# Expert products moved from split operands of 96 slots to plain fp32 in column groups of 128-slot rounds, with the final norm formed slot by slot

## The reference, cut to what matters

```python
lg = xt @ router_group;  le = xt @ router_expert        # group, then top 2 of its 8 experts
for e in range(N_EXPERTS):                              # 32 experts, D 1024, FF 256
    hdn = silu(xt @ w_gate[e]) * (xt @ w_up[e])
    y = y + comb[:, e:e + 1] * (hdn @ w_down[e])
y_prompt = rmsnorm(h + y, norm_final)[:, N_META:]       # and y_sample
```

## Time and profile before

| | us |
|---|---|
| median of 3 runs | 1011.46 (1009.23 to 1011.9) |
| the profiled execution, its own time | 1011.97 |
| its span, first to last instruction | 1010.1 |
| PE busy in the span | 917.7 |
| DVE busy | 595.2 |
| ACT busy | 503.5 |
| POOL busy | 234.6 |
| moved by DMA | 203.92 MB |

### The profile page before, as it was taken

One profiled execution on the slowest core, in us unless ns is written; L12 is line 12 of the kernel. 1 busy time (PEld: TensorE's weight loads), 2 busy tenths in 40 slices (PEclk: granted clock), 3 DMA queues, 4 the chain that ended last, 5 costly groups with the idle time before them and its releaser, 6 DMA issues. The chain is left out here.

```text
span 1010.1 us, 13905 instructions
## 1 busy us (share of the span) xinstructions
PE 917.7 (91%) x4971; PEld 725.2 (72%) x4971; DVE 595.2 (59%) x1051; ACT 503.5 (50%) x870; POOL 234.6 (23%) x304
## 2 busy tenths in 40 slices
PE   3899999999999999987899999499999999999962
PEld 3799887888878887775678776377777777777621
DVE  4503533253324432366685336888999999888756
ACT  4523344334443434334332212568888888888614
POOL 1102223233213322202452201211011011010435
PEclk9999999999999999998699999689999999999977
DMA  8032221321232122317145534999999999999976
GB/s 250 38 109 77 89 73 52 96 78 58 74 114 72 54 74 75 120 32 226 64 138 180 177 125 180 358 314 385 388 394 394 398 398 393 400 401 373 350 276 229
DMA packets 88363, 203.92 MB, mean 202 GB/s; under 512 B 11903, under 2 KB 55231, under 8 KB 76006
## 3 DMA queue, kind: packets, MB, share of 16 engines
q1 hardware_dynamic: 77806, 169.99, 47.4%
q0 software_dynamic: 5984, 17.18, 5.1%
q10 hardware_dynamic: 4504, 15.85, 4.1%
HBM read 167.02 MB, written 39.99 MB: 205 GB/s over the span
## 5 line engine op out<-in xcount | busy, mean ns | idle before, releaser
L1017 PE MATMUL pj<-n_hi,w_hi 128*128 128x350 f32 (+1 forms) x576 | 199.2, 346 | 3.5 <-DVE n_lo L1337 3.5
L1017 PE MATMUL pj<-n_lo,w_hi 128*128 128x350 f32 (+1 forms) x576 | 188.5, 327 | 0.0
L1017 PE MATMUL pj<-n_hi,w_lo 128*128 128x350 f32 (+1 forms) x576 | 187.6, 326 | 0.0
L1941 DVE TENSOR_TENSOR e_lo<-e_raw,e_hig 128x2048 fp32r<-128x2048 f32 x64 | 145.9, 2282 | 0.0
L1017 PEld LDWEIGHTS pj<-n_hi,w_hi 128*128 128x128 f32 x576 | 109.9, 191 | 35.4 <-issue 33.6
L1299 DVE CUSTOM_DVE_ANT_0 sc<-pj,strip 128x512 f32<-128x512 f32 (+5 forms) x120 | 60.9, 544 | 119.0 <-PE pj L1083 78.0
L1937 ACT ACTIVATE e_hig<-e_raw 128x2048 fp32r<-128x2048 f32 x64 | 122.5, 1918 | 10.3 <-DMA e_raw<-in_w_up 9.6
L1017 PEld LDWEIGHTS pj<-n_lo,w_hi 128*128 128x128 f32 x576 | 110.2, 191 | 0.6
L1017 PEld LDWEIGHTS pj<-n_hi,w_lo 128*128 128x128 f32 x576 | 109.8, 191 | 0.9 <-issue 0.8
L1989 PE MATMUL pj<-e_hig,xT_hi 128*96 128x512 f32 x256 | 104.8, 410 | 0.0
L1989 PE MATMUL pj<-e_hig,xT_lo 128*96 128x512 f32 x256 | 101.3, 396 | 0.0
(11 more groups left out here) (291 smaller groups left out, 1637.5 us busy)
## 6 DMA issues: line engine op xcount, KB each, us to landing
e_raw<-in_w_up SPq DMA_DIRECT2D x32, 1024.0 KB, 16.7
e_raw<-in_w_gate SPq DMA_DIRECT2D x32, 1024.0 KB, 20.7
e_raw<-in_w_down SPq DMA_DIRECT2D x32, 1024.0 KB, 21.2
w_raw<-in_w_in SPq DMA_DIRECT2D x24, 512.0 KB, 4.0
expert_rows<-yo ACTq DMA_DIRECT2D x32, 384.0 KB, 8.1
expert_rows<-logits SPq DMA_DIRECT2D x26, 384.0 KB, 4.6
wo_raw<-in_w_out SPq DMA_DIRECT2D x8, 512.0 KB, 5.2
k_page<-in_cache_k SPq DMA_DIRECT2D x16, 256.0 KB
```

What stands on the lines that cost most here:

```text
L1017: ins = pe.matmul(pj[g % 2][:, 0:tn], ws[w][:, P * k:P * (k + 1)], x[:, k, t0:t0 + tn], start=(m == 0), stop=(m == 23))
L1941: eng.tensor_tensor(e_lo[r][:, q, :], e_raw[r][:, q, :], e_hi(par, q).bitcast(F32), ALU.subtract).then_inc(s_lo[q], 1)
```

## The change

The 32 experts with 96 slots each are laid end to end in 24 rounds of 128 slots, so a round holds quarters (32 slots) of two experts. The high and low parts are gone from the expert stage: the products take `e_raw`, `xT` and `hT` in plain float32. Within a round each expert's slots are the columns of their own stationary tile, and the result goes to their own partitions. `pieces` makes one tile of 64 columns of two aligned quarters of one expert, else tiles of 32 columns:

```diff
-        RD = 4
+        RD = 5
+        def pieces(r):
+            runs, q = [], 0
+            while q < 4:
+                n = (4 * r + q) // 3
+                size = 2 if q % 2 == 0 and (4 * r + q + 1) // 3 == n else 1
+                runs.append((n, 32 * q, 32 * (q + size)))
+                q += size
+            return runs
...
             for k in range(k0, k1):
-                for a, (x, w) in enumerate(((xT_hi, e_hig[par]), (xT_hi, e_lo[r]), (xT_lo, e_hig[par]))):
-                    ins = pe.matmul(gu_bank[par][0:CB, :].rearrange("p (q f) -> p q f", q=2), x[:, par, k, :], w[:, 0:2, FF * k:FF * (k + 1)],
-                                    start=(k == 0 and a == 0), stop=(k == KC - 1 and a == 2))
+                for n, a, b in pieces(r):
+                    ins = pe.matmul(gu_bank[r % 2][a:b, :].rearrange("p (q f) -> p q f", q=2), xT[:, r % 2, k, a:b],
+                                    e_raw[n % RD][:, 0:2, FF * k:FF * (k + 1)], start=(k == 0), stop=(k == KC - 1))
...
-        def high(act, n, q, r, par):
-        def low(eng, n, q, r, par):
...
+        def gather_h(pool, r):
+            if r >= 2:
+                pool.wait_ge(s_back[r % 2], 16 * (r // 2))
+            if r >= 3:
+                pool.wait_ge(s_z, 2 * (r - 3) + 2)
+            gather(pool, hy[r % 3][:], h_dram, tab[:, r, 0:1], s_hy[r % 3])
+        def scatter_back(pool, r):
+            pool.wait_ge(s_z, 2 * r + 2)
+            scatter(pool, h_dram, TOK, tab[:, r, 1:2], zs[r % 2][:], s_back[r % 2])
+        def scatter_out(pool, r):
+            pool.wait_ge(s_fo, r - DONE0 + 1)
+            scatter(pool, y_out, SEQ, tab[:, r, 2:3], on[r % 2][:], s_out[r % 2])
+            scatter(pool, y_smp, DEC, tab[:, r, 3:4], on[r % 2][:], s_out[r % 2])
+        def dve_z(dve, r):
...
+                dve.scalar_tensor_tensor(zs[r % 2][:, part], dn[b][:], gate_s[:, r:r + 1], hy[r % 3][:, part], ALU.mult, ALU.add).then_inc(s_z, 1)
```

More of the change, by code:

```diff
@@ L1711, in route_place @@
             T = t1 - t0
+            high, past, at_p = (rks[:, i, :, t0:t1] for i in range(3))
+            dve.wait_ge(s_step, did.n[0])
+            did(dve.tensor_tensor(high, rk0[:, :, t0:t1], two(far[:, t0:t1], T), ALU.is_ge))
+            did(dve.tensor_tensor(at_p, rk0[:, :, t0:t1], two(home[:, t0:t1], T), ALU.add))
+            did(dve.tensor_scalar(past, rk0[:, :, t0:t1], float(CB), float(GONE), ALU.is_ge, ALU.mult))
+            dve.wait_ge(s_step, did.n[0])
+            did(dve.scalar_tensor_tensor(at_p, high, -float(P), at_p, ALU.mult, ALU.add))
@@ new lines, in tokens, with do, tables @@
+        def tokens(dve, did, M, found, n, n0, counted):
+            def do(ins):
+                did(ins)
+                dve.wait_ge(counted, did.n[0])
+            sf = slot_f[0:M, n0:n0 + n]
+            do(dve.tensor_scalar(sf, found, 0.0, float(GONE), ALU.is_equal, ALU.mult))
+            do(dve.scalar_tensor_tensor(sf, found, -1.0, sf, ALU.add, ALU.add))
+            do(dve.tensor_copy(tab[0:M, n0:n0 + n, 0], sf))
+        def tables(dve, did, M, last, gate, n, n0, counted):
+            def do(ins):
+                did(ins)
+                dve.wait_ge(counted, did.n[0])
+            sf = slot_f[0:M, n0:n0 + n]
+            notl, idx, low, row = ((tmp_t if n0 == 0 else tmp_x)[0:M, i, :] for i in range(4))
+            did(dve.tensor_copy(gate_s[0:M, n0:n0 + n], gate))
+            did(dve.scalar_tensor_tensor(idx, last, float(GONE), sf, ALU.mult, ALU.add))
+            do(dve.tensor_scalar(notl, last, -float(GONE), float(GONE), ALU.mult, ALU.add))
+            did(dve.tensor_copy(tab[0:M, n0:n0 + n, 1], idx))
+            do(dve.tensor_tensor(notl, notl, sf, ALU.add))
+            for i, first in ((2, META), (3, PROMPT)):
+                do(dve.tensor_scalar(low, sf, float(first), 2.0 * GONE, ALU.is_lt, ALU.mult))
+                do(dve.scalar_tensor_tensor(row, notl, -float(first), low, ALU.add, ALU.add))
+                do(dve.tensor_copy(tab[0:M, n0:n0 + n, i], row))
@@ L1862, in pe_r @@
                 for t in range(TE, NT):
-                    ins = pe.matmul(pj[1][0:CB, 0:NE], place_hot[:, c, t, :], block_tok[:, c, t, :], start=False, stop=(c == 1 and t == NT - 1))
+                    ins = pe.matmul(pj[1][:, 0:NRD], place_hot[:, c, t, :], place_tok[:, c, t, :], start=False, stop=(c == 1 and t == NT - 1))
+            ins.then_inc(s_pm, 1)
+            for c in range(2):
+                pe.wait_ge(s_ph, 4 + c + 1)
+                for t in range(NT):
+                    ins = pe.matmul(pj[3][:, 0:2 * NRD], place_hot[:, c, t, :].bitcast(F32), place_pay[:, c, t, :, :].rearrange("p a b -> p (a b)"),
+                                    start=(c + t == 0), stop=(c == 1 and t == NT - 1))
             ins.then_inc(s_pm, 1)
@@ L1957, in pe_xt, with experts_of, first_round, last_round @@
[L1957 to L1959 removed]
+        DONE0 = NG * CB // P
+        BACKS = [len(range(w, NRD, 2)) for w in range(2)]
+        OUTS = [len([r for r in range(w, NRD, 2) if r >= DONE0]) for w in range(2)]
+        def experts_of(r):
+            return sorted({(4 * r + q) // 3 for q in range(4)})
+        def first_round(n):
+            return 3 * n // 4
+        def last_round(n):
+            return (3 * n + 2) // 4
@@ new lines, in act_xt, with pe_gu @@
+                if r >= 2 and q == 0:
+                    act.wait_ge(s_gu, r - 1)
+                act.activation(xT[:, r % 2, 4 * q:4 * q + 4, :].rearrange("p c t -> p (c t)"), xb[q][:], ACT.Copy).then_inc(s_xte, 1)
+        def pe_gu(pe, r, k0, k1):
+            if k0 == 0:
+                pe.wait_ge(s_xte, 2 * r + 2)
+                for n in entering(r):
+                    for q in range(2):
+                        pe.wait_ge(s_er[3 * (n % RD) + q], 16 * (n // RD + 1))
+                if r >= 2:
+                    pe.wait_ge(s_hh, r - 1)
@@ new lines, in pe_dn @@
+        def pe_dn(pe, r):
+            pe.wait_ge(s_hte, r + 1)
+            for n in entering(r):
+                pe.wait_ge(s_er[3 * (n % RD) + 2], 16 * (n // RD + 1))
+            for b in range(2):
+                if r >= 1:
+                    pe.wait_ge(s_z, 2 * (r - 1) + b + 1)
+                for f in range(2):
+                    for n, p0, p1 in pieces(r):
+                        o = D * f + 512 * b
+                        ins = pe.matmul(dn[b][p0:p1, :], hT[:, f, p0:p1], e_raw[n % RD][:, 2, o:o + 512], start=(f == 0), stop=(f == 1))
+                ins.then_inc(s_dn, 1)
@@ new lines, in pool_m @@
+            for r in range(3):
+                gather_x(pool, r)
+            for r in range(2):
+                gather_h(pool, r)
+            pool.wait_ge(s_slots, 2)
+            for n in range(NRD + 2):
+                if n + 3 < NRD:
+                    gather_x(pool, n + 3)
+                if n >= 2:
+                    scatter_back(pool, n - 2)
+                if n - 2 >= DONE0:
+                    pool.wait_ge(s_sq, n - 2 - DONE0 + 1)
+                    root(pool, did, n % 2, s_pool)
+                    scatter_out(pool, n - 2)
+                if 2 <= n < NRD:
+                    gather_h(pool, n)
@@ L2225, in pe_m @@
             more_blocks(pe, body, lists)
-        RF = 4
-        o_s2 = r0 + 24576
-        f_h = [at(f"f_h{i}", [P, D], F32, r0 + 83456 + 4096 * i if i < 6 else r0 + 4096 * (i - 6)) for i in range(NT)]
-        f_a = [at(f"f_a{i}", [P, D], F32, (r_sc + 4096 * i + 128 * (i // 2)) if i < 3 else (r0 + 4096 * i) if i < 6 else o_s2 + 4096 * (i - 6))
-               for i in range(NT)]
-        f_b = [at(f"f_b{i}", [P, D], F32, r_o + 4096 * i if i < 6 else o_s2 + 4096 * (i - 3)) for i in range(NT)]
@@ L2412, in _ @@
             sp_m(sp)
-            sp_f(sp)
         @block.gpsimd
```

813 lines of the change are left out of this document (323 added, 490 removed).

## The result

The change makes the kernel slower: 1175.2 us (median of 4, 1172.66 to 1178.3) against 1010.35 for the kernel before beside it, a ratio of 1.1632 with a 95% interval of 1.1597 to 1.1667. The profiled execution has a span of 1170.8 us.

What follows compares the result with a forecast made beforehand. PE was taken as the bound, with DMA also near its end. Start 661.75 + rounds 503 + wait 1 + tail 12 = 1177.8; with 1.9 around the span 1179.7, and the profiled execution 0.5 above the median: 1179 us, range 965 to 1215.

Steps and rivals of the forecast that it cites:

- 64 and 32 columns side by side are two settings, 2.00 us a mixed step: Expert stage on PE: a step with tiles of both widths costs two visits of 1.00 us each; chance 0.60.
- 0.865 for a step of one shape: Expert stage on PE: equal tiles run side by side, so a step takes two passes, 0.865 us.
- rival 3: Expert stage on PE: nothing overlaps in a long stream, 64 tiles one after another, 1377 us; chance 0.05.
- 503 us for the rounds, and 1 for a wait at their end: 24 rounds on PE: 16 of 25.5 and 8 of 11.9 us, then hidden units wait once, +1.
- Start at 661.75: First expert product: 659.75 before, routing adds 2.5 us of small DVE steps and loses 0.5 for low parts.
- gates and tables come later, behind the first rounds' products: Start of the expert stage: gates and tables were placed after the first rounds' products, with no time at the start.
- Tail of 12 us: After the last matmul: z, square, root, norm, two scatters, landing of 5 and hand-overs sum to 12 us, replacing 41.
- DMA, POOL, DVE and ACT hidden: Expert stage: DMA's 292 us of 503, POOL's some 8 us a round, DVE's and ACT's 3 lie beside PE.
- Rival 1: Expert stage: mixed tiles overlap too, rounds cost 11.9 us on PE, DMA sets the pace, 985 us; chance 0.30.
- the trip through DRAM: Scatter of z and gather of `h` two rounds on: at most 24.5 us, against 42 us that two rounds take.

## Why the prediction was right, point by point

The forecast was 1179 us; measured are 1175.2. The mechanism is the one forecast, but that the total is so near is partly luck: the rounds came out 10 us below their term, the start 3 and the tail 0.6 above, and the median lies 4.4 above the profiled span where the forecast had 1.4.

- **64 and 32 columns side by side are two settings, 2.00 us a mixed step.** Measured 1.985. Shown: with one shape everywhere the 163 us are gone, a change costs 0.135 to 0.14 us, and what is left of a mixed step is two sets one after another. That this is a setting of the whole array is a reading that fits all runs; no run looks inside. The rule of the Trainium skill ("TensorEngine Tiling (Array Packing)", Key Properties, a change of tiling mode drains the engine) agrees with these runs: 0.135 us for each change, and sets of different width never together. The trace of before had no such step; the choice came from what weight loads do at a change of shape.
- **0.865 for a step of one shape.** Measured 0.895 as the mean of four steps between transposes; within them the weights come every 0.43 us, 0.86 a step. Line 1507 carried over to a long stream; rival 3 is out.
- **503 us for the rounds, and 1 for a wait at their end.** Measured 493.7, from 664.50 to 1158.2. The term was 2% high: three rounds are 62.9 in the sum and 61.7 in the trace. It counted every visit by itself, also where one product ends with the width that the next begins with. Of the 1.2 us, 0.97 is one place. Gate and up (2041) end there on two tiles of 32, down (2083) begins on two of 32 in the other columns, and all four run as one set, as PE's weight loads show:

```profile
796.10 0.11 PEld L2041 LDWEIGHTS pj<-e_raw,xT 128*32 128x32 f32 x2 [0.81 <-issue]
796.11 0.11 PEld L2083 LDWEIGHTS pj<-e_raw,hT 128*32 128x32 f32 x2
796.13 0.12 PEld L2041 LDWEIGHTS pj<-e_raw,xT 128*32 128x32 f32 x2
796.14 0.12 PEld L2083 LDWEIGHTS pj<-e_raw,hT 128*32 128x32 f32 x2
797.10 0.19 PEld L2083 LDWEIGHTS pj<-e_raw,hT 128*64 128x64 f32 x2 [0.84 <-issue]
```

The two other places where widths meet save a change each (down in 3.43 and 7.79 in place of 3.58 and 7.94). The kernel thus had tiles of two different products running together, if of one width, and the prediction hadn't looked for it.

- **Start at 661.75.** Measured 664.50. The step that failed is "gates and tables come later, behind the first rounds' products": they come ahead of them on PE, 7.9 us at the 1.2 GHz level. From the list's matmul to the first product it takes 16.0 us here (648.47 to 664.50), 11.9 before (line 1863 at 647.81, to 659.75), and 11.8 with the tables moved. So the tables cost 4 us; the rest of their 7.9 lies beside the landing of the first tokens. The list itself came only 0.7 us later than before, where the sum had 2; but line 1897 starts anywhere from 647.6 to 653.0 us in the runs here, behind the same stages, so that 0.7 says little.
- **Tail of 12 us.** Measured 12.6, from the last matmul's end at 1158.2 to 1170.8. It replaces the 41 of before. The sum hits it partly by luck: the last scatter back to `h_dram` stands ahead of the root on POOL (0.98 us), which had no term, and 1.4 us lie idle between the two scatters of output, but the span ends 3.6 us after the last issue where I had 5.
- **DMA, POOL, DVE and ACT hidden.** Right: PE is at 100% for 400 us, and the gather of `h` lands after 4.1 us in the middle.
- **Rival 1's price, 985 us, if shapes cost nothing.** Here the working was wrong. With one shape the kernel takes 1012. I had taken the trip through DRAM as 24.5 us for two rounds and added 11 for three limits together. Not named was what is queued behind the waiting gather on POOL, the next scatter; and the landings grow when DMA is full. Shown: without the trip the kernel takes 973, 35 us less from the routing on, and PE doesn't stop even with DMA at 405 GB/s. So it isn't bandwidth by itself that holds the rounds back, but landings that stand in a chain. That 973 is near rival 1's sum before its 11 (974) is luck in part: that sum counts the 4.3 MB that this run leaves out, 11 us. Open is how much of a landing in the chain is its own length and how much is load on DMA; neither fewer bytes nor held-back loads told them apart.

## What to carry to other kernels

Here tiles in column groups ran together only where they had the same width, also across two products; a step that mixed 64 and 32 paid for each width by itself. So cut all tiles to the smallest width: in this stream of 512 moving columns that cost nothing (3.57 us for four steps of four tiles, 3.58 for four steps of two). Before a change, look in the trace for the place that already does the new thing, and at what the engine does on the way into and out of it. And where a queue waits for a landing, follow the chain through what stands in front of the wait and behind it: to put the gather elsewhere in the queue gave 7 us and a new chain, to be without the trip 35.

## What the runs showed of the hardware

- Two float32 tiles or four in column groups keep their passes in step: all first passes, then 0.43 us later all second ones, with the weight loads of a set within 0.13 to 0.19 us. That holds in a stream as long as 32 records.
- A change of tile width costs 0.135 us in a stream (eight changes to two: 7.94 to 7.13 us), and 0.14 by the turned order (7.94 to 7.53). Tiles of 64 and 32 columns never overlap, though they touch different columns; tiles of one width do, even from two products (6.97 in place of 7.94 us).
- A gather of up to 128 rows of 4 KB (87 on average, 2096 rows in 24) lands after 4.1 us in the middle with DMA at 250 GB/s, 8.4 at 375, 10.1 at 385 with a longest of 17.7, and 12.9 at 405 with a longest of 18.7. With two weight loads in flight at most it is 8.3 at 354.
